# Three sum products for the feed-forward norm, a later sum for the final norm, and an output projection by turns in a two-block fp32 kernel

## What is computed

```
first block:  h = x + meta;  a = rms_norm(h);  z = a @ w_in            (1024 x 6144)
              mix = sigmoid(gate) * (attention @ w_na_out) + sigmoid(gate) * (recurrence @ w_hg_out)
              h = h + mix @ w_o                                        ("o")
              m = rms_norm(h);  h = h + square(relu(m @ w_up)) @ w_down ("up0".."up3", "down0".."down3")
              h = rms_norm(h)                                          ("fin")
even layer:   [a, v, ga, u, gb] = modulated norm of h @ even_in;  pooled part and gated part, times silu(gate)
              h = h + gate * (y @ even_out)                            ("eo0", "eo1")
odd layer:    [glr, qk, gv, gcd, sq/sk/sv] = modulated norm of h @ odd_in
              a gated linear attention with a norm per head ("go"), and a stick-breaking attention
              h = h + gate * (y @ odd_out), final norm
```

## Time and profile before

| | |
|---|---|
| time, median of 3 runs | 846.06 us (845.83 to 847.05) |
| the profiled execution | 853.3 us, of it 851.3 from the first to the last instruction |
| TensorE matmul busy | 834.7 us, 98% |
| VectorE, ScalarE, GpSimd busy | 631.0, 494.2 and 113.2 us |
| chain of waits that ended last | TensorE 97%, ScalarE 1%, DMA 1% |
| moved by DMA | 170.4 MB, 200 GB/s on average |

### The profile page before, as it was taken

How to read it: one execution, slowest core, us unless ns; L and a number is a source line. 1 busy time by engine, 2 the same in 40 slices (tenths; PEclk the granted TensorE clock), 3 DMA queues, 4 the chain that set the end, 5 groups by cost and what they waited for, 6 DMA issues and landing times.

```text
span 851.3 us, 16989 instructions
## 1 busy us (share of the span) xinstructions
PE 834.7 (98%) x6904; PEld 813.9 (96%) x6904; DVE 631.0 (74%) x1002; ACT 494.2 (58%) x878; POOL 113.2 (13%) x130
## 2 busy tenths in 40 slices
PE   5999999999999999999999999999999999999996
PEld 5998899997999999999999999999999999999996
DVE  5676578995896868686889798886788557655663
ACT  6454456663767555554666764554677366766652
POOL 0010254420121000000030430000202030000001
PEclk9999999999999999999999999999999999999999
DMA  9833343456666988889775676765656435655431
GB/s 358 312 106 115 115 146 110 149 166 206 190 187 208 305 321 280 342 282 386 230 252 188 216 216 220 260 198 175 202 152 187 123 109 174 212 156 154 144 103 50
DMA packets 46877, 170.40 MB, mean 200 GB/s; under 512 B 5201, under 2 KB 5457, under 8 KB 46545
## 3 DMA queue, kind: packets, MB, share of 16 engines
q1 hardware_dynamic: 46080, 165.31, 59.2%
q10 hardware_dynamic: 720, 4.01, 1.2%
HBM read 168.26 MB, written 1.05 MB: 199 GB/s over the span
## 4 chain that ended last, share of the span: by engine, by line
PE 97%; ACT 1%; DMA 1%; DVE 0%; SPq 0%; issue 0%; DVEq 0%; POOLq 0%; POOL 0%; ACTq 0%
PE bank L196 96%; DMA raw<-in_ws 1%; PE bank L199 0%; ACT wh L205 0%; SPq L193 0%; ACT sq L202 0%; DVE gc L235 0%; DVEq L335 0%; DVE h L223 0%; ACT vt L202 0%; ACT XUh L202 0%; POOLq L335 0%; POOL sq L235 0%; DVE wl L235 0%; DVE sq L235 0%
## 5 line engine op out<-in xcount | busy, mean ns | idle before, releaser
L235 DVE TENSOR_TENSOR wl<-raw,wh 128x1024 fp32r<-128x1024 f32 x259 | 325.2, 1268 | 22.7 <-ACT wh L205 21.7
L205 ACT CAST wh<-raw 128x1024 fp32r<-128x1024 f32 x259 | 268.9, 1048 | 112.2 <-PE bank L196 65.6
L196 PE MATMUL bank<-XAh,wl 128*128 128x256 f32 (+1 forms) x896 | 256.5, 286 | 0.0
L196 PE MATMUL bank<-XAl,wh 128*128 128x256 f32 (+1 forms) x896 | 251.0, 280 | 0.0
L196 PE MATMUL bank<-XAh,wh 128*128 128x256 f32 (+1 forms) x896 | 251.0, 280 | 0.0
L196 PEld LDWEIGHTS bank<-XAh,wl 128*128 128x128 f32 x896 | 168.4, 188 | 2.1 <-issue 1.8
L196 PEld LDWEIGHTS bank<-XAl,wh 128*128 128x128 f32 x896 | 170.3, 190 | 0.0
L196 PEld LDWEIGHTS bank<-XAh,wh 128*128 128x128 f32 x896 | 169.0, 189 | 0.1
L196 PE MATMUL bank<-B1h,wl 128*128 128x256 f32 (+1 forms) x464 | 131.1, 283 | 0.0
L196 PE MATMUL bank<-B1h,wh 128*128 128x256 f32 (+1 forms) x464 | 130.2, 281 | 0.0
L196 PE MATMUL bank<-B1l,wh 128*128 128x256 f32 (+1 forms) x464 | 130.2, 281 | 0.0
(11 more groups left out here) (261 smaller groups left out, 1236.5 us busy)
## 6 DMA issues: line engine op xcount, KB each, us to landing
raw<-in_ws SPq DMA_DIRECT2D x307, 512.0 KB, 4.3
bias<-in_bias ACTq DMA_DIRECT2D x1, 1664.0 KB, 11.5
hK<-in_xk SPq DMA_DIRECT2D x4, 272.0 KB, 4.6
h<-in_xt ACTq DMA_DIRECT2D x1, 1088.0 KB, 6.4
out<-gc SPq DMA_DIRECT2D x4, 256.0 KB, 2.6
C<-in_cst SPq DMA_DIRECT2D x1, 512.0 KB, 7.5
crow<-in_crow ACTq DMA_DIRECT2D x1, 512.0 KB, 3.4
wT<-in_wt SPq DMA_DIRECT2D x1, 512.0 KB, 5.8
```

The costliest lines, as they stand in the source:

```text
L196: return self.real.matmul(*a, **k)
L205: return self.real.copy(*a, **k)
L235: return self.real.tensor_tensor(*a, **k)
```

## The change

It takes "o" by turns; gives the "mlp" norm three products behind units 4, 5 and 6 of "up0" (GpSimd then adds squares 1 to 5 only); makes the "fin" sums behind units 1, 2 and 3 of "gb" instead of units 1 and 2 of "ga", with their logarithm and exponential behind "gb"; and puts one more side step ahead of the fourth "go" sum on TensorE, ScalarE, VectorE and GpSimd.

```diff
--- before.py
+++ after.py
@@ -42,7 +42,7 @@
 
 
 
-BY_TURNS = ("up0", "a", "qk")
+BY_TURNS = ("o", "up0", "a", "qk")
 
 
 def plan():
@@ -66,7 +66,7 @@
     mat("w_na_out", 0, 1024, nk=4)
     mat("w_in", 5632, 6144)
     mat("w_hg_out", 0, 1024, nk=4)
-    mat("w_o", 0, 1024)
+    mat("w_o", 0, 1024, two=True)
     mat("w_up", 0, 1024, two=True)
     for g in range(4):
         if g > 0:
@@ -791,9 +791,9 @@
                 if k == 7:
                     side.give(("sums", site), *freed)
 
-            def square_sums(site, last, *freed):
-
-                todo = [(5,), (6, 7)]
+            def square_sums(site, last, *freed, todo=((5,), (6, 7))):
+
+                todo = list(todo)
 
                 def go():
                     if todo and last in w.left:
@@ -958,17 +958,7 @@
             w.drain()
             t_tiles("hg", "w_hg_out", 0, 1024, (B0h, B0l),
                     lambda k: [("hg_high", k - 4), ("hg_low", k - 4)], lambda t: [("hg_mix", t)], nk=4, xk=4)
-            def mlp_sum():
-
-                if ("up0", 1) in w.left and sums:
-                    sums.clear()
-                    ps = side.take("sums", "mlp")
-                    e.wait_ge(*at("sq_add", ("mlp", 7)))
-                    e.matmul(ps[:, 0:256], cst_("ones"), sq_of("mlp", 0)[:, 0:256], start=True, stop=True).then_inc(
-                        *up("sums", ("mlp", 7)))
-                    side.give(("sums", "mlp"), ("rs", "mlp"))
-
-            sums.append(mlp_sum)
+            square_sums("mlp", ("up0", 1), ("rs", "mlp"), todo=((5,), (6,), (7,)))
             t_pairs("o", "w_o", 0, 1024, XA, lambda k: [("x2_high", k), ("x2_low", k)], lambda t: [("h_o", t)], main)
 
             def up_tiles(g, c0, c1, t0=0):
@@ -998,7 +988,6 @@
 
             w.side.append(pool_side())
             t_rows("vn", "even_in", 2048, 3072, X, X_of("even"), lambda b, col: [("vn", (col, b))], HALVES)
-            square_sums("fin", ("vn", 512), ("rs", "fin"))
 
             def pool_product(n):
                 j = unit_of["pool_w", 4 * n, 0]
@@ -1039,7 +1028,9 @@
             t_tiles("u", "even_in", 1536, 2048, X, X_of("even"), lambda t: [("zu", t)], t0=4)
             pool_product(1)
             w.drain()
+            square_sums("fin", ("u", 7), ("rs", "fin"), todo=((5,), (6,), (7,)))
             t_tiles("gb", "even_in", 4096, 5120, X, X_of("even"), lambda t: [("silu", ("gb", t))])
+            sums.clear()
             t_tiles("eo0", "even_out", 0, 1024, (B0h, B0l), lambda k: [("ya0_high", k), ("ya0_low", k)],
                     lambda t: [("h_eo", (0, t))])
             square_sums("odd", ("eo1", 7), ("rs", "odd"))
@@ -1102,6 +1093,7 @@
                     side.give(("go", hh), ("go_copy", hh))
                     yield
                     yield
+                yield
                 go_sum(3)
                 for r in range(2):
                     side.give(("gsum", r), ("go_rs", r))
@@ -1245,12 +1237,12 @@
                 sq_at[site, k] = n
                 if k == 0:
                     return
-                if k < 6 or site == "mlp":
+                if k < 6:
                     squares.give(n, ("sq_add", (site, k)))
                 else:
                     squares.give(n, ("sums", (site, k)))
                 if k == 7:
-                    squares.give(sq_at[site, 0], ("sums", (site, 7 if site == "mlp" else 5)))
+                    squares.give(sq_at[site, 0], ("sums", (site, 5)))
 
             def rsqrt(site, ps, N, after, rs=rsB):
                 e.wait_ge(*at(*after))
@@ -1601,7 +1593,6 @@
                         *up("vn_rs", "ln"))
                     e.wait_ge(*now("vn_rs"))
                     e.activation(ss[:, :, 5:6], ss[:, :, 4:5], ACT.Exp, scale=-0.5).then_inc(*up("vn_rs", "rs"))
-                    rsqrt("fin", bk("sums", "fin")[:, 0:256], 256, ("sums", ("fin", 7)))
                     table(EXP_SET)
                 silu("ga")(ts)
 
@@ -1632,6 +1623,8 @@
                         yb0_high(t - 2)
 
             tiles("gb", "even_in", 4096, 5120, gb_out)
+            table(LN_SET)
+            rsqrt("fin", bk("sums", "fin")[:, 0:256], 256, ("sums", ("fin", 7)))
 
             def eo0_out(ts):
                 if ts[0] == 0:
@@ -2542,7 +2537,7 @@
                 def leave(ts):
                     for site in sites:
                         for t in ts:
-                            if 1 <= t < (8 if site == "mlp" else 6):
+                            if 1 <= t < 6:
                                 a, b = sq_of(site, 0), sq_of(site, t)
                                 e.wait_ge(*at("sq", (site, t)))
                                 if t > 1:
```

## The result

The changed kernel takes 843.51 us (median of 20 runs, 842.54 to 844.71) against 847.14 us for the kernel before (median of 20 runs beside it, 843.08 to 854.18). The ratio is 0.9947, with a 95% interval of 0.9928 to 0.9967: faster by half a per cent, not by the one per cent of the forecast (837.4 us). The recorded execution took 844.48 us (span 842.7), 8.8 us less than the one of the kernel before. So the recorded executions give the forecast's 8.7 us and the medians do not. That is the riddle of this case.

A forecast was written before the change was run, and what follows sets the result against it. TensorE, 98% busy, was taken as the bound, so only its own stream counts. Terms -0.28 - 7.6 + 0.87 + 0 - 1.3 - 0.4 = -8.7 us, from 846.06, gave 837.4 us; own range 835.5 to 840, with two rivals 835.5 to 845.2.

The forecast's parts named there:

- the last of the sum: Whole kernel: the profiled-to-median difference of 7.2 us also applies after the change, so 846.06 - 8.7 gives 837.4 us.
- the -7.6 us: "o" and feed-forward: fast pace kept through 1692 products, 4.5 ns each, gains 7.6 us; bounds 0 and -7.6.
- the unprofiled runs are fast already: Rival, chance 0.07: the wait in "o" exists only under the profiler; the change adds its two products, 846.9 us.
- the "go" step: Fourth "go" sum one unit later: its 0.04 us wait goes, 287 products stay fast, -1.3 us; bounds 0 and -1.3.
- The reading of the switch: TensorE's stream: pace, fast or slow, survives a sum product on time; a wait of even 40 ns drops it to slow.
- the signs that the prediction named: Profile after: no interval above 0.12 us in "o"; some 179 instead of 172 products per 20 us through "down3".
- The wait in "o": Second unit of "o", waiting for VectorE's `XAl`: taking it by turns removes the wait, -0.28 us.
- Two more "mlp" sums: Feed-forward norm in "up0": two added sum products cost 0.43 us each, in full on the path, +0.87 us.
- "fin": Final norm's three sums, moved behind "gb" units: each keeps the pace it finds, 0; "gb", "eo0", "eo1" stay slow.
- ScalarE's block behind "gb": Logarithm, exponential and table load at the end of "gb": some 2.3 us, covered by 2 us, 0; bounds 0 to +1.
- The slower rival: Rival, chance 0.05: ScalarE's block behind "gb" delays high parts, low parts and VectorE's queue; 849.0 us.
- "a": First tiles of the even layer, 258 columns, 194 products: partly faster, -0.4 us, between 0 and -0.9.

The follow-up runs named there:

- the third recording: The kernel before, unchanged, recorded again in a later job for another trace: 846.57 us.
- the first recording: The kernel before, unchanged, the profiled execution on which the prediction was made: 853.3 us, with a span of 851.3 us.

## Why the prediction was wrong, and where it was right

**The step that failed** is the last of the sum: "That is 7.2 us above the median of the unprofiled runs; I apply the same difference to that". The recorded execution belonged to a quarter of the executions, the one with the slow feed-forward. The other three quarters had the fast pace already (the third recording shows it, same wait included: 113.5 ns per product in the feed-forward), so the -7.6 us was there to be had only in the quarter. That was the rival "the unprofiled runs are fast already", given 0.07, with its argument written beside it: the two figures are as large as each other. In one thing it was off as well: it took the slow pace for something that the recording does. The unrecorded executions have both groups too, and among the recorded ones the wait is there with the feed-forward at 113.5 ns and at 117.8 ns alike. And its price, 846.9 us, left out the "go" step.

**The reading of the switch** was half right. There are two paces, an on-time product keeps the fast one, and a wait can drop it. But a wait does not always drop it: the one in "o" (0.31 us from start to start) left the stream slow in five traces and fast in two. In the changed kernel the wait of 0.7 us in "ga" left it fast and the one of 0.14 us slow. And the slow pace is not for good: a sum sometimes lifts it, a tiny product every time. Of the signs that the prediction named, the feed-forward has its 179 products in 340 to 360 us, and no interval in "o" is above 0.12 us.

**The terms**, with the third recording of before (846.57 us) against that of the changed kernel (844.48), by the starts of the units' last products. A negative number means that the changed kernel is faster:
- The wait in "o": -0.29 us (forecast -0.28).
- Its pace: 0 in three executions of four, -7.5 in the others (forecast -7.6): from 237.4 to 438.6 us the first recording takes 201.17 us for the products for which the third takes 193.68. So the size was right; what failed is the choice of the executions it applies to.
- Two more "mlp" sums: +0.92 (forecast +0.87), the same against the trace with a single sum.
- "fin", forecast 0, is the other term that was wrong, in two ways. In "ga" 1.3 us of products left and 0.86 us came back as the two waits for VectorE: -0.44, and +0.09 behind it. What was late next had not been looked for there. In "gb" the sums cost 1.3 but, in this execution, lifted the pace: +0.85 in the eight units with the sums, then -0.85, -0.85 and -0.23 through "eo1". In all -1.4 us, by a mechanism that the prediction excluded ("each keeps the pace it finds"; "gb", "eo0" and "eo1" "as slow as before").
- ScalarE's block behind "gb" is hidden, as forecast. The slower rival did not come.
- The "go" step: -0.77 - 0.35 = -1.1 (forecast -1.3): the pace was fast for 260 products, not 287, since the rows of `sv` dropped it at 716 us. The kernel before, slow ahead of the same rows, is fast in them (last section), so part of the gain went back there.
- "a": 0 (forecast -0.4). The forecast's 118.5 ns came of a wrong count: three sums are six records, so the stretch of the earlier trace rows has 197 - 6 = 191 products, and 22.99 / 191 = 120.4 ns, as now (120). 258 columns take about 120 ns whatever precedes them.

These and -0.1 at the start make -1.9 us (the +0.09 behind "go" included), and 846.3, the middle of the main group, less 1.9 is 844.4; the changed kernel's median is 843.5, probably because some of its executions keep the fast pace behind the waits in "ga" too, as the recorded one with a single "mlp" sum does.

That the two first recorded executions differ by 8.6 us of span, next to the forecast's 8.7, is partly luck: -1.4 for "fin" makes up for the 0.7 us by which the changed kernel's was later all the way up to "o", the 0.4 that "a" did not bring and the 0.2 missing at "go".

**The rule of the skill.** The Trainium skill, "TensorE: Matmul & The Clock Gate", section "Back-to-back issue gap", gives columns / 2.4 + 2.5 ns for an isolated matmul with a warm clock, which makes 109 ns for 256 columns (an estimate from that page), and beside it one sustained figure for a column count, about 81 ns for 128 and 131 ns for 512. The prediction left out that its formula is meant for the isolated one. All traces at the full granted clock here show 113.4 or 117.8 ns for 256 columns, both in one program at one place. By one gap for each column count none of the gains in pace could exist.

## What to carry to other kernels

Compare the recorded execution's own time with the spread of the unrecorded ones before costing anything on it: if it lies in another group, a term read from it holds for that group alone. Look at the single runs and not only the median, and record again until each group has a trace. Where TensorE is the bound, read its pace from start to start. A slow stretch behind a wait can be made fast by a plain product of 2 columns at 0.22 us, but only as far as the next wait or the next change between streaming tokens and streaming weights, and the gain is lost if TensorE then runs into an engine that had just kept up.

## What the runs showed of the hardware that was not expected

- One and the same program takes 842, 846, 850 or 854 us at a granted clock of 1.00, by the pace (113.4 or 117.8 ns per product of 256 columns) that two places leave behind, the wait in "o" and waits of hundredths in "ga" (842 and 850 by inference from the "go" step's recording).
- What a wait leaves is not fixed. Every trace has one more, at the sum of the last norm (827 to 840 us): 1.06 us instead of 0.67 from the product ahead of the sum to the second one behind it. The stream came in fast in all 19 traces at the full clock, and went out fast in 6 and slow in 13. What decides is open.
- A plain product of 2 columns that came on time made a slow stream fast in 10 of 10 cases (one of them right behind a sum) and kept a fast one in 11 of 11. A single sum of 256 columns kept a fast stream in every case where it came on time, but lifted a slow one in 3 of 15 (at 535.08 in the changed kernel, 267.07 in the one without turns, and 267.63 in the kernel before with two tiny products, far ahead of these), not counting the three in "u" that stood beside other plain products and lifted nothing. Why 2 columns do better is open.
- The pace also changes with no wait at all where the operands exchange roles, and there it is no matter of chance. At some 476 us (483 behind a slow feed-forward) fast rows, weights streaming, are followed by slow tiles, tokens streaming, in 19 of 19 traces at the full clock. At the first `sv` rows (713 to 726 us) the pace turns over: the 12 streams that came in fast went on slow, the 7 that came in slow went on fast. The rows of the changed kernel (5.78 / 49 = 118.0 ns, behind tiles at 113.4) and of the third recording of before (5.68 / 50 = 113.6, behind tiles at 117.9):

```profile
716.80:722.30 5.50, 5.50 (x49) 1.00 0.94 348
```
```profile
718.90:724.30 5.40, 5.40 (x50) 1.00 0.91 281
```

- One execution ran at a granted clock of 0.75 from end to end, 1034 us; TensorE in 20 us of it:

```profile
300.00:320.00 20.00, 20.00 (x143) 0.75 0.51 163
```
